# Depthwise convolution on one Trainium2 core: first tap to ScalarE, gate to GpSimd, three slots fewer for the taps, and a new order of the blocks behind them

## What is computed

```
h = xn @ w_in + b_in                       # 2048 -> 3 * 2048
a, g, z = jnp.split(h, [CONV_WIDTH, 2 * CONV_WIDTH], axis=-1)
u = a * jax.nn.sigmoid(g)
u = conv(u, dw, 31 taps, depthwise, padding 15) + dw_b
mu = jnp.mean(u, axis=-1); var = jnp.mean((u - mu)**2, axis=-1)
u = silu((u - mu) * rsqrt(var + LN_EPS) * ln_g + ln_b)
y = (u * silu(z)) @ w_out + b_out
```

## Time and profile before

| | us |
|---|---|
| median of 3 runs | 883.33 (883.22 to 883.35) |
| the profiled execution's own time | 884.47 |
| its span (first to last instruction) | 882.4 |
| TensorE busy | 867.9 (98% of the span) |
| VectorE busy | 575.2 (65%) |
| ScalarE busy | 444.2 (50%) |
| GpSimd busy | 204.6 (23%) |

### The profile page before, as it was taken

One profiled execution on the slowest core, in us unless ns is written; L12 is line 12 of the kernel. 1 busy time (PEld: TensorE's weight loads), 2 busy tenths in 40 slices (PEclk: granted clock), 3 DMA queues, 4 the chain that ended last, 5 costly groups with the idle time before them and its releaser, 6 DMA issues.

```text
span 882.4 us, 11845 instructions
## 1 busy us (share of the span) xinstructions
PE 867.9 (98%) x4674; PEld 739.3 (84%) x4674; DVE 575.2 (65%) x906; ACT 444.2 (50%) x568; POOL 204.6 (23%) x58
## 2 busy tenths in 40 slices
PE   7999999999999999999999999999999999989997
PEld 7998899889988899888888888888888888867885
DVE  6556554584457554576455545998888899498661
ACT  7745443456335633557444544445434564766532
POOL 0000000000000000000000007877787778651000
PEclk8999999999999999999999999999999999999999
DMA  9976455545554465444555554555555455536702
GB/s 335 394 263 213 161 192 191 191 161 173 180 187 148 156 222 191 165 169 135 198 174 172 174 196 150 184 191 167 171 188 189 162 176 189 188 98 234 256 34 96
DMA packets 97846, 163.59 MB, mean 185 GB/s; under 512 B 3296, under 2 KB 38368, under 8 KB 97288
## 3 DMA queue, kind: packets, MB, share of 16 engines
q1 hardware_dynamic: 96320, 160.77, 54.2%
q10 hardware_dynamic: 1480, 2.19, 0.7%
HBM read 160.83 MB, written 3.69 MB: 186 GB/s over the span
## 4 chain that ended last, share of the span: by engine, by line
PE 95%; DVE 3%; ACT 1%; DMA 1%; issue 0%
PE ps_acc L1118 23%; PE ps_acc L1120 23%; PE ps_acc L1121 23%; PE ps_acc L1135 7%; PE ps_acc L1138 7%; PE ps_acc L1137 7%; PE ps_a L1081 2%; PE ps_d L1081 1%; DMA sb_vec_all<-in_vectors 1%; DVE sb_w_lo L739 0%; PE ps_a L1202 0%; PE ps_a L1201 0%; PE ps_a L1200 0%; DVE sb_conv_lo L1002 0%; PE ps_d L1179 0%; PE ps_d L1178 0%
## 5 line engine op out<-in xcount | busy, mean ns | idle before, releaser
L431 ACT ACTIVATE sb_w_hi<-sb_w_raw 128x2048 fp32r<-128x2048 f32 x141 | 269.8, 1915 | 304.1 <-PE ps_acc L1121 220.0
L739 DVE TENSOR_TENSOR sb_w_lo<-sb_w_raw,sb_w_hi 128x2048 fp32r<-128x2048 f32 x97 | 222.1, 2291 | 162.6 <-ACT sb_w_hi L431 162.4
L422 POOL TENSOR_TENSOR sb_w_lo<-sb_w_raw,sb_w_hi 128x2048 fp32r<-128x2048 f32 x44 | 203.0, 4615 | 96.4 <-ACT sb_w_hi L431 96.4
L1118 PE MATMUL ps_acc<-sb_w_hi,sb_conv_hi 128*128 128x512 f32 x512 | 205.4, 401 | 3.0 <-DVE sb_conv_lo L1002 3.0
L1120 PE MATMUL ps_acc<-sb_w_lo,sb_conv_hi 128*128 128x512 f32 x512 | 202.8, 396 | 0.0
L1121 PE MATMUL ps_acc<-sb_w_hi,sb_conv_lo 128*128 128x512 f32 x512 | 202.7, 396 | 0.0
L939 DVE SCALAR_TENSOR_TENSOR ps_d<-sb_uT,sb_dwT,ps_d 128x256 f32<-128x256 f32 x480 | 190.0, 482 | 0.0
L1118 PE MATMUL ps_acc<-sb_w_hi,sb_act_hi 128*128 128x512 f32 x384 | 152.3, 397 | 0.0
L1121 PE MATMUL ps_acc<-sb_w_hi,sb_act_lo 128*128 128x512 f32 x384 | 151.4, 394 | 0.0
L1120 PE MATMUL ps_acc<-sb_w_lo,sb_act_hi 128*128 128x512 f32 x384 | 151.4, 394 | 0.0
L1135 PE MATMUL ps_acc<-sb_act_hi,sb_w_hi 128*128 128x256 f32 x512 | 144.9, 283 | 3.1 <-DVE sb_w_lo L775 3.1
(11 more groups left out here) (153 smaller groups left out, 612.3 us busy)
## 6 DMA issues: line engine op xcount, KB each, us to landing
sb_w_raw<-in_attn_w_in SPq DMA_DIRECT2D x61, 1024.0 KB, 5.3
sb_w_raw<-in_conv_w_in SPq DMA_DIRECT2D x64, 512.0 KB, 4.5
sb_w_raw<-in_attn_w_out SPq DMA_DIRECT2D x16, 1024.0 KB, 5.0
sb_w_raw<-in_conv_w_in SPq DMA_DIRECT2D x16, 1024.0 KB, 5.0
sb_w_raw<-in_conv_w_out SPq DMA_DIRECT2D x16, 1024.0 KB, 5.1
sb_w_raw<-in_attn_w_in SPq DMA_DIRECT2D x6, 512.0 KB, 8.0
sb_xT<-in_x_turned SPq DMA_DIRECT2D x4, 512.0 KB, 8.0
sb_xs<-in_x SPq DMA_DIRECT2D x2, 1024.0 KB, 16.0
```

The costliest lines, as they stand in the source:

```text
L422: pool.tensor_tensor(w_lo[slot][:], w_raw[slot][:], w_hi[slot][:].bitcast(F32), ALU.subtract).then_inc(lo_ready_pool, 1)
L431: act.activation(w_hi[slot][:], w_raw[slot][:], ACT.Copy).then_inc(hi_ready, 1)
L739: dve.tensor_tensor(w_lo[slot][:], w_raw[slot][:], w_hi[slot][:].bitcast(F32), ALU.subtract).then_inc(lo_ready, 1)
L1118: pe.matmul(into, left_hi, w_hi[i][:, k], start=(kt == 0 and not filled), stop=False, skip_group_check=filled)
```

## The change

Five things are edited.

1. The gate leaves VectorE. ScalarE writes `a + b` into a new SBUF tile `a_rows` (an extra Identity activation before the Sigmoid, L296 of the new file), and GpSimd multiplies (`gate`, L430), in its program ahead of a chunk's low part: two gates before every four low parts, 16 in all. ScalarE's Sigmoid now frees the PSUM bank.
2. The first tap leaves VectorE: `first_tap` on ScalarE (L673), two activations a pair, with scale and bias.
3. VectorE keeps 30 taps a pair, spread over slots 6 to 41 in place of 6 to 44. All that is placed by the taps' end (last copy, last turn, LayerNorm statistics, broadcast) stands three slots earlier: the broadcast halfway through slot 43.
4. On ScalarE the block steps, which stood after the loop over the slots, are put into the iterations of slots 43 to 46, and the last `h_out` stands in the iteration of slot 47 behind them.
5. On VectorE the block steps have another order: gates first, then the low parts in twos.

```diff
-        CONV_START, CONV_END = 6, LATE - 4
-        STEPS = [(pair, tap) for pair in range(KT // 2) for tap in range(TAPS)]
+        CONV_START, CONV_END = 6, LATE - 7
+        STEPS = [(pair, tap) for pair in range(KT // 2) for tap in range(1, TAPS)]
...
+                if k >= 2:
+                    act.wait_ge(gate_done, k - 1)
+                act.activation(a_rows[:, k % 2], bank_a[0][:, 0:SEQ], ACT.Identity, bias=vecs[:, B_A, k:k + 1]
+                               ).then_inc(gate_ready, 1)
                 act.activation(uT[:, k, HALO:HALO + SEQ], bank_a[0][:, SEQ:2 * SEQ], ACT.Sigmoid,
-                               bias=vecs[:, B_G, k:k + 1]).then_inc(gate_ready, 1)
+                               bias=vecs[:, B_G, k:k + 1]).then_inc(a_free, 1)
...
+            def gate(n, f):
+                k = 2 * n + f
+                row = uT[:, k, HALO:HALO + SEQ]
+                pool.wait_ge(gate_ready, k + 1)
+                pool.wait_ge(a_free, 2 + A_CONV + FILLS.index(("ag", n, f)) + 1)
+                pool.tensor_tensor(row, a_rows[:, k % 2], row, ALU.mult).then_inc(gate_done, 1)
+            for c in range(POOL_FROM, POOL_TO):
+                n, f = divmod(c - POOL_FROM, NCH)
+                if n < Z_FROM and f < 2:
+                    gate(n, f)
+                pool.wait_ge(hi_ready, c + 1)
+                pool.tensor_tensor(w_lo[c % RING][:], w_raw[c % RING][:], w_hi[c % RING][:].bitcast(F32),
+                                   ALU.subtract).then_inc(lo_ready_pool, 1)
...
+            def first_tap(pair):
+                if pair == 0:
+                    act.wait_ge(taps_landed, 16)
+                    act.wait_ge(d_free, 2 + D_X1 + SPLITS)
+                elif pair >= 2:
+                    act.wait_ge(v_ready, pair - 1)
+                act.wait_ge(gate_done, 2 * pair + 2)
+                for e in range(2):
+                    k = 2 * pair + e
+                    act.activation(bank_d[pair % 2][:, e * SEQ:(e + 1) * SEQ], uT[:, k, 0:SEQ], ACT.Identity,
+                                   scale=dwT[:, k, 0:1], bias=vecs[:, DW_B, k:k + 1]).then_inc(tap0_done, 1)
...
-            silus(0)
-            block_hi(0)
...
+            for i in range(LN_SLOT + 1, LATE):
+                hi_of(CHUNKS_OUT + i + RING)
+                if i % NCH == NCH - 1:
+                    h_out(i // NCH)
+                for kind, n, f in fills_at.get(i, ()):
+                    empty_conv_fill(act, kind, n, f)
+                if i == LATE - 5:
+                    silus(0)
+                    silus(1)
+                if i == LATE - 4:
+                    block_hi(0)
+                    silus(2)
+                    block_hi(1)
+                    silus(3)
...
+                if i == LATE - 2:
+                    block_hi(4)
+                    silus(6)
+                    block_hi(5)
+                    silus(7)
             empty_conv_fill(act, *fills_at[LATE][0])
```

More of the change, by code:

```diff
@@ L153, in build @@
             uT = sb("uT", [P, KT, PADW], F32, one)
+            a_rows = sb("a_rows", [P, 2, SEQ], F32, one)
             h_rows = sb("h_rows", [P, ST, GW], F32, one)
@@ L204, in build @@
         halo_clear = sem("halo_clear")
-        gate_ready = sem("gate_ready")
+        gate_ready, gate_done, tap0_done = sem("gate_ready"), sem("gate_done"), sem("tap0_done")
         tap_done = sem("tap_done")
@@ L646, in h_out @@
                                    ).then_inc(acc_free, 1)
+            def first_tap(pair):
[9 more added lines that the diff above has]
+                                   scale=dwT[:, k, 0:1], bias=vecs[:, DW_B, k:k + 1]).then_inc(tap0_done, 1)
+            v_slot = {pair: i for i, pair in v_at.items()}
+            gated_at = {NCH * (pair + 1) + 2: pair for pair in range(KT // 2)}
             for i in range(LN_SLOT + 1):
+                if i in gated_at and v_slot.get(gated_at[i] - 2, 0) < i:
+                    first_tap(gated_at[i])
                 hi_of(CHUNKS_OUT + i + RING)
@@ L655, in _ @@
                     pair = v_at[i]
-                    act.wait_ge(tap_done, 2 * TAPS * (pair + 1))
+                    act.wait_ge(tap_done, 2 * (TAPS - 1) * (pair + 1))
                     act.activation(uT[:, 2 * pair:2 * pair + 2, 0:SEQ],
@@ L660, in _ @@
                                    ).then_inc(v_ready, 1)
+                    if pair + 2 <= LAST and NCH * (pair + 3) + 2 <= i:
+                        first_tap(pair + 2)
                 if i in turn_at:
@@ L667, in _ @@
                     load_table(ACT.Silu)
-            silus(0)
-            block_hi(0)
[L672 to L684, removed]
+            for i in range(LN_SLOT + 1, LATE):
[12 more added lines that the diff above has]
+                    silus(3)
+                if i == LATE - 3:
+                    block_hi(2)
+                    silus(4)
+                    block_hi(3)
+                    silus(5)
+                if i == LATE - 2:
[3 more added lines that the diff above has]
+                    silus(7)
             empty_conv_fill(act, *fills_at[LATE][0])
-            block_hi(5)
-            silus(7)
             block_hi(6)
@@ L921, in step @@
             def step(pair, tap):
-                s = pair * TAPS + tap
+                s = pair * (TAPS - 1) + tap - 1
                 for e in range(2):
@@ L925, in step @@
                     out_ = bank_d[pair % 2][:, e * SEQ:(e + 1) * SEQ]
[L926 to L936, removed]
+                    if tap == 1:
+                        dve.wait_ge(tap0_done, 2 * pair + 2)
                     else:
                         dve.wait_ge(tap_done, 2 * s + e - 1)
-                        dve.scalar_tensor_tensor(out_, src, dwT[:, k, tap:tap + 1], out_, ALU.mult, ALU.add
-                                                 ).then_inc(tap_done, 1)
+                    dve.scalar_tensor_tensor(out_, uT[:, k, tap:tap + SEQ], dwT[:, k, tap:tap + 1], out_, ALU.mult,
+                                             ALU.add).then_inc(tap_done, 1)
             def as_diagonal(dst, col):
@@ L946, in as_diagonal @@
                                             ALU.mult)
[L948 to L954, removed]
             for i in range(LN_SLOT):
@@ L959, in _ @@
                     low_part(c, c % RING)
[L960 to L966, removed]
+                for pair, tap in steps_at.get(i, ()):
                     step(pair, tap)
@@ L1008, in _ @@
             gate_block(0)
-            block_lo(0)
             normalise(2)
             gate_block(1)
[L1012 to L1017, removed]
+            normalise(3)
+            gate_block(2)
+            normalise(4)
+            gate_block(3)
+            normalise(5)
+            block_lo(0)
+            block_lo(1)
+            normalise(6)
+            block_lo(2)
+            gate_block(4)
+            block_lo(3)
+            normalise(7)
+            gate_block(5)
+            block_lo(4)
+            block_lo(5)
+            gate_block(6)
+            block_lo(6)
+            gate_block(7)
+            block_lo(7)
             def with_bias(n, st, dst):
```

## The result

The changed kernel takes **886.94 us** (median of 6 runs, 886.50 to 888.11) against 883.32 us before: ratio 1.0043, 95% interval 1.0033 to 1.0053, so 0.4% slower. The forecast was 887.4, 4.1 us more than before; the median moved by 3.6.

What follows compares the result with a forecast made beforehand. TensorE, busy 867.9 of 882.4 us, was taken as the bound. Removing the old wait (-4.8) and adding a new wait with its clock loss (+8.9) gave +4.1: 887.4 us, own range 886.4 to 889.5, 8 in 10 879.5 to 890.

Steps and rivals of the forecast that it cites:

- What there is to win: TensorE's 3.13 us wait between the halves of C0 plus 1.66 us at the lower clock behind it: 4.8 us.
- Moved work costs nothing: Slots 4 to 34: gates on GpSimd (0.6 to 0.8 us) and first taps on ScalarE (0.41 us) cost TensorE nothing.
- Three slots earlier: The first normalise on VectorE comes at 754.3, 17.7 us earlier, while C0 begins where it did.
- The chain: VectorE's gates and low parts of blocks stand behind GpSimd's low parts, holding ScalarE; the last h_out ends at 793.2.
- The new wait: TensorE waits 7.2 us for the last h_out at the fill behind C0, from 786.0 to 793.2.
- The clock: Lower clock on TensorE behind that fill costs between 1.7 and 2.7 us; 1.7 taken.
- The sum: Old wait and its clock -4.8 us, new wait and its clock +8.9: net +4.1 us, median 887.4 us.
- get past GpSimd: Rival: gate 1 and low part 2 asked for before GpSimd starts; up to 4.8 us won, 878.5 to 880.5; chance 0.17.
- become the bound: Rival: GpSimd gates over 1.9 us delay low parts, TensorE waits in slots 8 to 36; 890 to 895; chance 0.05.

Runs made afterwards that it cites:

- e6: The kernel of e1 with the emptying of the fill behind C0 also moved up on ScalarE, ahead of silus 7: 878.07 us.
- e4: The changed kernel with GpSimd's low parts of the last six chunks it serves cut from 2048 elements to 64: 878.13 us.
- e8: The kernel before, gates and first taps left on VectorE, taps three slots shorter, with the block orders of e6: 878.53 us.
- e3: The changed kernel with only the moved gate and first tap: taps spread up to slot 44, both block orders put back to before's: 883.14 us.
- e1: The changed kernel with the last h_out moved on ScalarE ahead of block_hi 4: 878.95 us.
- e7: The changed kernel with GpSimd's low parts of the last six chunks made by four instructions of 512 elements each: 883.75 us.
- e2: The changed kernel with VectorE's block steps in the order of before: 892.08 us.
- e5: The changed kernel with 30 multiplies of the tile of ones, result unused, on TensorE ahead of the fill behind C0: 885.39 us.

## Why the prediction was right

By its own steps:

- *What there is to win.* Forecast 4.8 us. e6, e4 and e8 have a rest time of 352.05 to 352.11, 4.93 to 4.99 less than before. The missing 0.1 to 0.2 is a small delay at the fill behind C1 in the trace of before (the matmul behind that fill starts 0.58 us after it, where 0.35 passed behind C0's), which the sum left out.
- *Moved work costs nothing.* Right, by e3. GpSimd's gate takes 0.64 to 0.75 us in the changed kernel's trace; forecast 0.6 to 0.8. ScalarE's first tap takes 0.57 us, not the 0.41 that I took from a fill of z (0.46 by its own duration), and the added Identity 0.45. It had no effect.
- *Three slots earlier.* The first normalise was forecast at 754.3 and came at 752.03. The trace of the change runs 2.33 us ahead by its start, so that is 754.36 on the time axis of before.
- *The chain.* On the same time axis, forecast against measured: gate 0 asked for at 761.3, 761.30; gate 1 at 766.3, 766.07; low part 0 at 775.2, 775.07; low part 2 at 781.5, 781.36; GpSimd's low part ahead of it at 780.2, 779.86; end of h_out 793.2, 792.86. All collisions up to `h_out` took place, and no other. Behind it gate 6 stood too (1.81 us), and nobody waited for it.
- *The new wait.* Forecast 7.2, measured 7.0 in the list of waits, 7.2 from when the fill was due (783.50). That h_out's place is what carries it to TensorE is shown by e1; that GpSimd's instructions are what delays the gates by e4 and e7; that VectorE's new order was not the fault by e2.
- *The clock.* The least certain term is "I take 1.7, as the nearer stage". In the traced execution it was too small: 2.45 from fill to fill, and 2.4 against e5's trace. By the medians it was not: 886.94 - 878.07 (e6) - 7.17 of wait leaves 1.7, and e5's median lies 1.55 below the change's. So 1.7 fits the medians and is 0.75 short for the traced execution. The ground given for it, that the nearest stage is the best guess, the traces do not bear out: behind the still longer wait of e2 it was 1.3.
- *The sum.* Forecast +4.1; the rest times say +4.63, the medians +3.6. In the traces the clock's term is 0.75 larger, and against it stands the small delay of 0.2 that went and is not in the sum. That the median came within 0.5 us is in part luck: for the profiled execution, which the sum starts from, I forecast 888.6, and it took 886.50, with a start that was 2.33 us shorter. The range of 886.4 to 889.5 is also wider than its own terms, which give 883.33 - 4.8 + 6.7 + 1.7 = 886.9 to 883.33 - 4.8 + 8 + 2.7 = 889.2; the result lies at the lower end of these.
- *Rivals.* The gates did not get past GpSimd; the point named for it, low part 2 against GpSimd's start, was missed by 1.5 us (forecast 1.3), and gate 1 against GpSimd's start by 1.26 (forecast 1.3). GpSimd did not become the bound: in the changed kernel its low parts still wait 34.8 us for high parts, where they waited 96.4, and its gates wait 50.9 us for ScalarE.

## What to carry to other kernels

When a chain of steps is put into an earlier place of an in-order program, list what stands behind it on the same engine and by when each is wanted. In the changed kernel the chain itself was in time; a short step for another consumer, put behind it, was not. Make short work for GpSimd where VectorE has to work on two SBUF inputs, since what counts there is the length of one GpSimd instruction and not its load: in e7 its low parts took longer in sum (210.2 us against 203.3), and the kernel was 3.2 us faster than the change. And if a change has many parts, try each alone: here a constant and the order of steps, tried only together (e8), held all of the gain, and the moved work none.

## What the runs showed of the hardware that I had not expected

**A wait costs more than its length, and in the traces the extra does not follow the length.** Behind a wait of 3.0 us TensorE ran at the lower level until about 789.9, 3.7 us after it resumed (before); behind 7.0 us until about 796.0, 5.3 us (the change); behind 3.6 us until about 791.3 and behind 11.5 us, the longest, until about 800.2, some 2.7 us each (e7 and e2, which resume at 788.55 and 797.54). In the stretches of e2:

```profile
798.00:800.00 2.00, 2.00 (x7) 1.71 (x7) 0.40 (x1) 0.84 (x2) 2.00 (x1) 0.50 0.00 0
800.00:802.00 2.00, 2.00 (x9) 1.58 (x9) 1.41 (x1) 0.56 (x1) 0.86 (x1) 0.93 0.10 7
```

So one such wait costs its length and, in these four traces, 1.3 to 2.5 us more. The medians spread less. From each I take e6's median (878.07, where TensorE does not wait) and the wait's length in the trace, from when the next matmul was due:

| kernel | wait, us | extra in the one trace | estimate from the medians |
|---|---|---|---|
| before | 3.1 | 1.7 | 1.8 |
| e7 | 3.8 | 1.3 | 1.9 |
| the change | 7.2 | 2.45 | 1.7 |
| e2 | 11.7 | 1.3 | 2.3 |

The last column is an estimate, good to some tenths: e5, whose trace shows no lower clock, comes out at 0.15 by the same sum. With one trace of each kernel it stays open how much of the spread between the traces is of the kernels and how much of the single executions.

**The starts differ from trace to trace.** The first weight matmuls ran at a mean clock of 0.50 (before, e2, e8), 0.66 to 0.68 (e1, e4 to e7) or 1.00 (the change, e3) in 9 to 14 us, and slot 4's fill started between 523.03 and 525.38. The three traces with 0.50 are the latest (525.35 to 525.38), but the clock there is not all of it: e3 with 1.00 comes at 524.51, later than e1 with 0.67 at 524.32, and in e3 TensorE waits once for VectorE's `sb_o_rows` in the attention for 1.5 us, in the change for 0.6. Single executions of one kernel differ by as much (the kernel before: 882.64 to 884.50 in 21 runs), while its medians of 6, 15 and 21 runs lie at 883.32, 883.30 and 883.24.

**GpSimd stands behind VectorE too.** In e4 a GpSimd operation of 64 elements, 0.32 us elsewhere, takes 0.86 where it starts together with the first of two low parts of blocks on VectorE (769.81 to 771.22), and one at 775.86 takes 0.60 beside a gate:

```profile
769.81 0.86 POOL L439 TENSOR_TENSOR sb_w_lo<-sb_w_raw,sb_w_hi 128x64 fp32r<-128x64 f32 x1 [5.71 <-ACT sb_w_hi L449]
```

This is the other direction of the rule that the prediction quoted from the Trainium skill ("SBUF — State Buffer", section "SBUF: two separate sides"), which no row of the kernel before showed.
